# A pooling mixer at the start of a four-layer network: pooled means as products, and its norms by token halves

## The reference, cut to what matters

```
h = rms_norm(x, mix_pre_g[0])
for gi, w in enumerate((2, 4, 8, 16)):              # groups of 256 channels
    mean = trailing sum of h over w tokens / min(t, w)   # t = 1..512
    d[gi] = mean - h
y = einsum('bsgc,gcd->bsgd', d, w_pool) * pool_scale     # a 256x256 product in each group
x = x + rms_norm(y, mix_post_g[0])
f = conv_glu_ffn(rms_norm(x, ffn_pre_g[0]), ...)         # 1024 -> 5632 -> conv -> gated 2816 -> 1024
x = x + rms_norm(f, ffn_post_g[0])
```

## Time and profile before

| | us |
|---|---|
| median of 3 runs | 2565.0 (2564.91 to 2568.99) |
| the profiled execution, whole | 2566.03 |
| its span | 2564.3 |
| busy in the span: PE / PEld / DVE / ACT / POOL | 2349.7 / 1966.1 / 1450.6 / 1061.7 / 491.0 |
| mean granted clock of TensorE | 0.964 |

### The profile page before, as it was taken

One profiled execution on the slowest core, in us unless ns is written; L12 is line 12 of the kernel. 1 busy time (PEld: TensorE's weight loads), 2 busy tenths in 40 slices (PEclk: granted clock), 3 DMA queues, 4 the chain that ended last, 5 costly groups with the idle time before them and its releaser, 6 DMA issues.

```text
span 2564.3 us, 33874 instructions
## 1 busy us (share of the span) xinstructions
PE 2349.7 (92%) x12722; PEld 1966.1 (77%) x12722; DVE 1450.6 (57%) x1972; ACT 1061.7 (41%) x1511; POOL 491.0 (19%) x437
## 2 busy tenths in 40 slices
PE   2699999797889999878798999999999999999998
PEld 2487887675778788767678888888877778988887
DVE  5576578667567857767934533426656652542333
ACT  3454454335555444444234422325446652331331
POOL 3322122232233313224611000011001211000001
PEclk9799999899989999989899999999999999999999
DMA  3154453122225455424311222222211112222221
GB/s 132 47 193 176 175 191 145 66 99 66 83 83 197 166 164 190 154 113 170 128 66 66 103 94 98 99 90 85 101 66 35 52 51 82 99 91 92 96 98 66
DMA packets 55624, 280.06 MB, mean 109 GB/s; under 512 B 7916, under 2 KB 18928, under 8 KB 27616
## 3 DMA queue, kind: packets, MB, share of 16 engines
q1 hardware_dynamic: 33424, 211.45, 22.7%
q0 software_dynamic: 12560, 58.80, 6.6%
q10 hardware_dynamic: 9536, 8.39, 1.0%
HBM read 262.75 MB, written 15.86 MB: 109 GB/s over the span
## 4 chain that ended last, share of the span: by engine, by line
PE 73%; DVE 14%; ACT 5%; issue 4%; POOL 3%; DMA 0%; ACTq 0%; DVEq 0%; POOLq 0%
PE ps L443 21%; PE ps L444 20%; PE ps L445 20%; DVE w_lo L1705 3%; POOL sqsum L2639 2%; ACT w_hi L1034 2%; PE ps L937 1%; PE ps L938 1%; PE ps L939 1%; POOL gl L2720 1%; DVE v L2332 1%; PE ps L971 1%; DVE tg L1770 1%; DVE ada_w L1713 1%; PE ps L710 1%
## 5 line engine op out<-in xcount | busy, mean ns | idle before, releaser
L443 PE MATMUL ps<-h_hi,w_hi 128*128 128x512 f32 (+1 forms) x1984 | 735.5, 371 | 31.7 <-DVE w_lo L1705 17.9
L444 PE MATMUL ps<-h_lo,w_hi 128*128 128x512 f32 (+1 forms) x1984 | 727.3, 367 | 0.0
L445 PE MATMUL ps<-h_hi,w_lo 128*128 128x512 f32 (+1 forms) x1984 | 726.8, 366 | 0.0
L1705 DVE TENSOR_TENSOR w_lo<-raw,w_hi 128x2048 fp32r<-128x2048 f32 x194 | 445.5, 2297 | 465.0 <-ACT w_hi L1034 464.7
L1034 ACT ACTIVATE w_hi<-raw 128x2048 fp32r<-128x2048 f32 x194 | 370.8, 1912 | 387.4 <-PE ps L445 385.1
L443 PEld LDWEIGHTS ps<-h_hi,w_hi 128*128 128x128 f32 x1984 | 381.6, 192 | 102.4 <-issue 17.0
L443 PE MATMUL ps<-a_hi,w_hi 128*128 128x512 f32 (+1 forms) x1164 | 428.7, 368 | 31.3 <-DVE f L2148 14.4
L444 PEld LDWEIGHTS ps<-h_lo,w_hi 128*128 128x128 f32 x1984 | 381.9, 193 | 58.4 <-issue 1.0
L445 PEld LDWEIGHTS ps<-h_hi,w_lo 128*128 128x128 f32 x1984 | 381.8, 192 | 58.4
L444 PE MATMUL ps<-a_lo,w_hi 128*128 128x512 f32 (+1 forms) x1164 | 424.9, 365 | 0.0
L445 PE MATMUL ps<-a_hi,w_lo 128*128 128x512 f32 (+1 forms) x1164 | 424.9, 365 | 0.0
(11 more groups left out here) (382 smaller groups left out, 2671.1 us busy)
## 6 DMA issues: line engine op xcount, KB each, us to landing
raw<-weights_dram SPq DMA_DIRECT2D x161, 1024.0 KB, 4.8
ada_w<-ada_dram POOLq DMA_DIRECT2D x48, 1024.0 KB, 5.1
raw<-weights_dram SPq DMA_DIRECT2D x32, 704.0 KB, 3.9
par<-par_dram SPq DMA_DIRECT2D x8, 1152.0 KB, 7.1
par_dram<-plane POOLq DMA_DIRECT2D x10, 512.0 KB, 3.9
tab<-tab_dram SPq DMA_DIRECT2D x8, 512.0 KB, 5.8
x<-x_in_dram SPq DMA_DIRECT2D x1, 2048.0 KB, 8.9
par_dram<-bt_re ACTq DMA_DIRECT2D x4, 512.0 KB, 3.6
```

The source lines that it names most:

```text
L443: nc.tensor.matmul(dst, w_hi[:, o:o + P], rhs_hi, start=start, stop=False)
L444: nc.tensor.matmul(dst, w_hi[:, o:o + P], rhs_lo, start=False, stop=False)
L445: return nc.tensor.matmul(dst, w_lo[:, o:o + P], rhs_hi, start=False, stop=last)
L1705: nc.vector.tensor_tensor(w_lo[:, o], raw[:, o], w_hi[:, o].bitcast(f32), SUB).then_inc(w_split, 1)
```

## The change

Tokens first: `x_rows`, the input with tokens on the partitions, is loaded in four blocks of 128 tokens ahead of all else; `x` follows behind the first weight tile. ACT squares a block and sums it over its 1024 channels in one operation (`accum_out`), takes the root; VectorE inverts it and scales with it a constant band matrix (128 tokens by 144, for each window: 1/w on the trailing diagonals minus one on the main one; another version for the first 16 tokens). TensorE multiplies each block's 128 channels by that band: f32 products into eight banks, one for each chunk, of which the last 16 columns reach into the next block. The result is d without its channel gain; ACT and VectorE apply the gain as they split it into `dd_hi` and `dd_lo`.

The pooling products run by token halves (256 columns), four groups of half 0, then four of half 1, one bank for each group. The squares of the mix and of `x` are summed on TensorE directly: `start_sum` takes two 128x128 blocks of one squared half chunk by a column of ones, 32 such sums in four norms (m0, x0, m1, x1), in place of POOL's adds. Post norm and the norm of `x` run by halves, and the FFN's first two tiles use `in_pair` with the second half's sums threaded through (`FIRST_HALF`). POOL's two loads wait for the vectors; `cond`'s Silu and the Exp for S5 stand behind the last split of h on ACT. Weights of the pooling tile are split in four parts.

```diff
@@ SP
+        tokens(0)
+        sp.dma_start(band[:, :], consts[:, BAND:BAND + 4 * BW + 64]).then_inc(sem("band_landed"), 16)
+        sp.dma_start(vec[:, 0:gains], vecs[:, 0:gains]).then_inc(sem("band_landed"), 16)
+        for b in range(1, NB):
+            tokens(b)
...
             if name == "pool":
+                sp.dma_start(ident[:, :], consts[:, 0:P]).then_inc(sem("ident_landed"), 16)
+                sp.dma_start(x[:, :], x_in).then_inc(sem("vec_landed"), 16)
+                sp.dma_start(vec[:, gains:], vecs[:, gains:]).then_inc(sem("vec_landed"), 16)
+                sp.dma_start(posi[:, :], pos_in).then_inc(sem("tables_landed"), 16)
...
@@ TensorE
+        def start_sum(name, h, c, b0):
+
+            pe.wait_ge(sem("start_act"), START_STEP[f"{name}_sq{c}"])
+            for b in range(2):
+                o = c % 2 * T + h * TH + b * P
+                last = nc.tensor.matmul(bank(b0 + b, 1), sq[:, o:o + P], ones[:, 0:1], start=(c == 0), stop=(c == DC - 1))
+            last.then_inc(sem("start_pe") if c < DC - 1 else norm_sum_done, 1)
...
+        FIRST_HALF = {**{(0, 0, c + 1): m1_sum(c) for c in range(7)}, (1, 0, 0): m1_sum(7), (1, 0, 2): spread_of[1],
+                      **{(1, 0, c + 3): x1_sum(c) for c in range(5)}, (0, 1, 0): x1_last}
...
+            in_pair((name, name), (2, 2), h_hi, h_lo, hb, LATE_HALF if layer else FIRST_HALF)
...
-        norm_whole()
+        for c in range(DC):
+            nc.tensor.matmul(bank(c), zero_r[:, 0:P], zero_r[:, :], start=True, stop=False)
+        for b in range(NB):
+            pe.wait_ge(sem("start_dve"), START_STEP[f"band{b}"])
+            n = BW if b < NB - 1 else P
+            for c in range(DC):
+                o = c // 2 * BW
+                last = nc.tensor.matmul(bank(c, n, off=b * P), x_tok[:, b * D + c * P:b * D + (c + 1) * P], band_tok[b][:, o:o + n],
+                                        start=False, stop=(b == NB - 1))
...
+        for grp in range(4):
+            mixed(grp, 0)
+            if grp >= 2:
+                for c in (2 * grp - 4, 2 * grp - 3):
+                    start_sum("m0", 0, c, NORM)
+        for c in range(4, DC):
+            start_sum("m0", 0, c, NORM)
+        pe.wait_ge(sem("ident_landed"), 16)
+        for grp in range(4):
+            mixed(grp, 1)
+            if grp == 0:
+                spread_of[0]()
+        for c in range(DC):
+            start_sum("x0", 0, c, SUMS)
+        spread_of[0]()
...
@@ ScalarE
+        for b in range(NB):
+            act.wait_ge(sem(f"tok_landed{b}"), 16)
+            at = start_step(f"sq{b}", nc.scalar.activation(sq[:, :], x_tok[:, b * D:(b + 1) * D], ACT.Square, accum_out=tok_ss[:, b:b + 1]))
+            act.wait_ge(sem("start_act"), at)
+            start_step(f"std{b}", nc.scalar.activation(rcol[:, b:b + 1], tok_ss[:, b:b + 1], ACT.Sqrt, bias=EPS_A, scale=1.0 / D))
...
+        for c in range(DC):
+            act.wait_ge(sem("start_pe"), START_STEP[f"d{c}"])
+            nc.scalar.activation(chunk(dd_hi, c), bank(c), ACT.Identity, scale=v("mix_pre", c)).then_inc(sem("pool_dhi"), 1)
+        split_hi()
+
+        def mixed_square(name, h, c, src, **scaled):
+
+            if c >= 2:
+                act.wait_ge(sem("start_pe"), START_STEP[f"{name}_sum{c - 2}"])
+            start_step(f"{name}_sq{c}", nc.scalar.activation(halved(sq, c % 2, h), src, ACT.Square, **scaled))
...
+        for grp in range(4):
+            act.wait_ge(sem("start_pe"), START_STEP[f"mixed{grp}"])
+            for m in range(2):
+                mixed_square("m0", 0, 2 * grp + m, bank(grp, TH, off=m * TH), scale=v("pool_scale", 2 * grp + m))
+        mixed_copy(0, 0)
+        start_std(0, NORM)
+        for grp in range(1, 4):
+            mixed_copy(grp, 0)
+        for c in range(4):
+            x_square(0, c)
+            mixed_copy(c, 1)
+        x_square(0, 4)
+        g.after()
+        split_hi()
+        for c in range(5, DC):
+            x_square(0, c)
+        start_std(0, SUMS)
+        for c in range(DC):
+            split_halves(0, (c,), h_hi)
+            mixed_square("m1", 1, c, halved(f, c, 1))
+        start_std(1, SUMS)
+        for c in range(DC):
+            x_square(1, c)
+        start_std(1, SUMS)
+        split_halves(1, range(DC), h_hi)
+        act.wait_ge(sem("vec_landed"), 32)
...
@@ VectorE
+        for b in range(NB):
+            dve.wait_ge(sem("start_act"), START_STEP[f"std{b}"])
+            dve.wait_ge(dve_step, mark(nc.vector.reciprocal(rcol[:, b:b + 1], rcol[:, b:b + 1])))
+            ins = nc.vector.tensor_scalar(band_tok[b][:, :], band[:, 0:4 * BW], rcol[:, b:b + 1], None, MUL)
...
+        for c in range(DC):
+            if c % 2 == 0:
+                pool_w_lo(c // 2)
+            dve.wait_ge(sem("pool_dhi"), c + 1)
+            nc.vector.scalar_tensor_tensor(chunk(dd_lo, c), bank(c), v("mix_pre", c), chunk(dd_hi, c).bitcast(f32), MUL, SUB).then_inc(pool_d, 1)
+        split_lo()
+        g.after()
...
+        rstd_of(0)
+        rstd_on_all()
+        post_halves(0, range(DC), mix_gain, 0)
         split_lo()
+        rstd_of(0)
+        rstd_on_all()
...
+        norm_half(0, ffn_gain, h_hi, h_lo)
+        rstd_of(1)
+        rstd_on_all()
+        post_halves(1, range(DC), mix_gain, 4)
+        rstd_of(1)
+        rstd_on_all()
+        norm_half(1, ffn_gain, h_hi, h_lo)
...
@@ GpSimd
+        gp.wait_ge(sem("vec_landed"), 32)
+        gp.dma_start(cond[:, :], c_row).then_inc(sem("c_landed_ada"), 16)
         gp.dma_start(ada_w[:, :], ada[0:P, :]).then_inc(ada_landed, 16)
-        norm_adds()
-        norm_adds()
-        norm_adds()
```

More of the change, by code:

```diff
@@ L88 @@
 ONE_ROWS = HEAD_SEL + 8 * P
+BAND = ONE_ROWS + P
+BW = P + 16
 Q5 = 4
@@ L100, with eight @@
 START = {"mod_kept": 1, "xbc_done": 3}
+def eight(name, n=8):
+    return tuple(f"{name}{c}" for c in range(n))
+START_STEP = {name: k + 1 for names in (
+    ("sq0", "std0", "sq1", "std1", "sq2", "std2", "sq3", "std3", "w_hi0", "w_hi1", "w_hi2")
+    + eight("m0_sq") + eight("x0_sq") + eight("m1_sq") + eight("x1_sq"),
+    eight("d") + eight("mixed", 4) + eight("m0_sum", 7) + eight("x0_sum", 7) + eight("m1_sum", 7) + eight("x1_sum", 7),
+    eight("band", 4) + eight("w_lo", 3)) for k, name in enumerate(names)}
 FULL, FA, FB, XA, XB = "full", "fa", "fb", "xa", "xb"
@@ L144, in rounds, with build @@
         c.r, c.per, c.n = None, 0, c.n0 + n * per
-def build(nc, weights, ada, c_row, vecs, consts, x_in, pos_in, s5_b, s5_c, out):
+def build(nc, weights, ada, c_row, vecs, consts, x_in, x_rows, pos_in, s5_b, s5_c, out):
     f32, f32r, i32 = mybir.dt.float32, mybir.dt.float32r, mybir.dt.int32
@@ L610, in _, with mixed @@
         pe.wait_ge(sem("ones_set"), 1)
-        pe.wait_ge(sem("ident_landed"), 16)
-        norm_whole()
-        pe.wait_ge(w_split, g.after())
-        for grp in range(4):
-            if grp >= 2:
-                pe.wait_ge(pool_out, grp - 1)
+        for c in range(DC):
[7 more added lines that the diff above has]
+                                        start=False, stop=(b == NB - 1))
+                if b == NB - 1:
+                    last.then_inc(sem("start_pe"), 1)
+        def mixed(grp, h):
+            if h:
+                pe.wait_ge(pool_out, grp + 1)
+            elif grp < 3:
+                pe.wait_ge(sem("start_dve"), START_STEP[f"w_lo{grp}"])
+            else:
+                pe.wait_ge(w_split, g.after())
             for m in range(2):
@@ new lines, in start_std, with x_square @@
+        def start_std(h, b0):
+            act.wait_ge(norm_sum_done, C["norm"].after())
+            dst = rcol[:, 2 * h:2 * h + 2].rearrange("p (a o) -> p a o", o=1)
+            nc.scalar.activation(dst, as3(ps[:, b0 * T:(b0 + 2) * T], 2)[:, :, 0:1], ACT.Sqrt, bias=EPS_A).then_inc(std_done, 1)
+        def x_square(h, c):
+            act.wait_ge(x_ready, C["x"].after())
+            mixed_square(f"x{h}", h, c, halved(x, c, h))
+        for grp in range(4):
+            act.wait_ge(sem("start_pe"), START_STEP[f"mixed{grp}"])
+            for m in range(2):
+                mixed_square("m0", 0, 2 * grp + m, bank(grp, TH, off=m * TH), scale=v("pool_scale", 2 * grp + m))
@@ L1782, in norm_half, with post_halves @@
             C["hp"].after(DC)
-        def post_halves(h, chunks, gains):
+        def post_halves(h, chunks, gains, out_at=None):
             steps = []
@@ new lines, in pool_w_lo @@
+        def pool_w_lo(grp):
+            if grp < 3:
+                dve.wait_ge(sem("start_act"), START_STEP[f"w_hi{grp}"])
+            else:
+                dve.wait_ge(w_hi_done, split.after())
+            o = slice(grp * T, (grp + 1) * T)
+            ins = nc.vector.tensor_tensor(w_lo[:, o], raw[:, o], w_hi[:, o].bitcast(f32), SUB)
+            ins.then_inc(sem("start_dve") if grp < 3 else w_split, 1)
+        for c in range(DC):
+            if c % 2 == 0:
+                pool_w_lo(c // 2)
+            dve.wait_ge(sem("pool_dhi"), c + 1)
```

(8 more changed lines are left out.)

159 lines of the change are left out of this document (55 added, 104 removed).

## The result

The changed kernel takes 2539.8 us (median of 4 runs, 2539.4 to 2545.3) against 2566.3 for the kernel before on the same chip: ratio 0.990, interval 0.988 to 0.992, 26.5 us faster. The forecast was 2536 in a range of 2527 to 2553.

A forecast was written before the change was run, and what follows sets the result against it. TensorE's dense stream of products behind a slow start was taken as the bound. The third tile moving from 123.3 to 93.9 saves 29.4 us: 2566.0 to 2536.6, less 1.0 for the median, say 2536; eight in ten 2527 to 2553.

The forecast's parts named there:

- the third tile: Third FFN tile's first product, the yardstick: at 93.9 us instead of 123.3, 29.4 us earlier.
- Input, band products, d: Start: first tokens land at 4.5 us, band 0 ready at 8.4, band products end at 19, d's subtractions at 25.6.
- The wait for the second weight tile: Pooling: tile lands at 25 us, its split takes 1.91, so squares of the pooled output begin at 26.9.
- First norm: Norm of x's first half, ahead of the FFN: reaches VectorE at 50.5 us, against 94.83 before.
- rival (b): TensorE stays at 1.2 GHz through the start: 2562; cold only to x's norm: 2543. Chance 0.15 for 2547 to 2570.
- The mixed stretch: First FFN tile's first half, products with sums between: two chunks at 2.17 us, six at 1.2, ending at 63.7.
- Behind it: Second half's post steps start at 66.2 us, its products at 78.3; third tile 15.57 later; halves cost 43.4 us.
- ACT's late table loads: Exp, Silu and their loads behind h's last split: 3.8 us from 82.0, hidden with 0.5 to spare.
- The rest of the program: From the third tile to the span's end: 2441.0 us as before, within 2 us.
- (c): ACT's squares and TensorE's sums take turns: in addition to a cold start, 19 us more, 2581; chance 0.05.
- (d): The start doesn't set the end because the stream behind hides it: 2565; chance 0.02.
- (a): Clock high and tile early: weights at 23, no cold first sums or FFN chunks: 2529, range 2522 to 2529; chance 0.12.

The follow-up runs named there:

- second profile: Profile from running the changed kernel again, unaltered; it shows an execution of 2539.1 us, where that run's median was 2542.8 us.
- The fifth run: Changed kernel with the second-half mix squares in eight buffers of their own and their sums together behind the first half's FFN products: 2535.1 us, ratio 0.988.
- its repeat: The kernel with the second-half mix sums together behind the first half's FFN products, run again unaltered on the chip of the fillers: 2537.2 us, ratio 0.989.
- the two fillers: Kernel with the second-half mix sums taken out from between FFN products, plus seven idle f32 product pairs there: one column 2549.4 us, 128 columns 2544.0 us.
- front alone: Changed kernel's token blocks and band products, with pooling products, POOL's adds, norms and FFN of the kernel before: 2534.2 us, ratio 0.988.
- halves alone: Front of the kernel before, followed by the change's halves with sums on TensorE and interleaved FFN start: 2575.0 us, ratio 1.0035.
- the wide fillers: Kernel with the second-half mix sums taken out from between FFN products, plus seven idle pairs of 128-column f32 products there: 2544.0 us, ratio 0.991.

## Why the prediction was right, and where it was off

**Sign, size and place held, the size in part by luck.** 26.5 us measured, 29.4 forecast, and the gain lies in the start: 19.0 of the 20.6 us between the two profiled spans stand ahead of the third tile. At that tile, though, the forecast had 29.4, and the two profiles of the change have 19.0 and 23.0. In the second one, whose time of 2539.1 is near the median of 2539.8, 3.8 us more came from behind the tile, where the prediction expected nothing.

**Input, band products, d: right at both ends.** Tokens' first square at 4.75 (forecast 4.5), band 0 ready at 9.1 (8.4), band products through at 19.5 (19), d's first copy at 18.04 (17.2, to 22.3; measured to 22.8), last low half at 25.9 (25.6). In between, the second block of tokens was 2.5 us late, and the low clock lasted to 14 us where the prediction let it end at 12.3. The band's scaling was priced from an operation of another kind, 0.77, and took 0.52.

**The wait for the second weight tile: right.** Landed 24.9 (23.6 in the second profile), forecast 25 between 23 and 27; squares at 26.74, forecast 26.9. The chain of waits names it (DMA of raw from 8.61 for 16.29 us, then the split). That this wait decides was too much said: without it the time changes by 0 to 3 us.

**First norm: right on the mean, open in its cause.** 50.5 forecast, 54.5 and 49.5 measured in two executions of one program, with a granted clock of 0.56 and 0.89 from 26 to 41. I took the low clock for the first sums and a high one from 33.8. The fifth run, its repeat and the two fillers, whose program is the same up to there, have 0.77, 0.54, 0.77 and 0.66. What decides it in one execution isn't settled; the share of rival (b) that says cold up to the norm of x, 7 us late, is what the first profile shows by 4 us.

**The mixed stretch: the term that was mis-sized.** The prediction took two chunks at 2.17 and six at 1.2, 11.5 us, from the second layer, where the clock rises some 4.4 us into the products. Measured: every chunk 2.13, 16.4 us. The price of a cold chunk was right and the clock's rise was not: in the second layer no such sums stand between the products. The fillers show that the one-column sums are the reason. It is rival (b)'s price for this one stretch; (b) as a whole, 1.2 GHz through the start and 2562, did not come: the records run at the high price from 14 to 26 us, and the clock was at 0.97 from 41 to 48 and from 75 to 84.

**Behind it** the intervals held: from VectorE's second post norm to the second half's products 12.7 us (forecast 12.1), from there to the third tile 15.1 (15.6), with the one wait of 1.8 us for w_lo. The halves cost 50 us (49.7 and 50.8 in the two profiles) from VectorE's first product of the norm to the third tile, where 43.4 was charged and the whole form needs 28.4. The prediction had this sum in hand and didn't draw its consequence, that the halves might be worth less than they cost; no rival took the change apart in that way. The runs did: front alone 30.0 us faster, halves alone 10.1 slower, both 21.3 faster.

**ACT's late table loads: right.** Exp and Silu ran from 92.87 to 96.77, the tile's own table load followed at 96.84, and nothing waited. The root started 0.02 us behind the end of its table load (5.91 + 1.28, then 7.21), as in the earlier trace rows. The Trainium skill ("ScalarE: Activation LUTs", "What ACT_TABLE_LOAD costs") would have each switch drain for about 1380 ns more; this trace again doesn't show it.

**The rest of the program** was expected to be equal within 2 us. The first profile keeps to that, the second, by the prediction's own sign, doesn't: from the third tile to the end 2441.0 us before, and 2437.2 to 2440.2 in the twelve profiles after, 2439.5 and 2437.2 in two of the same kernel. This gave back 1.5 to 3.8 us of the miss in front. Only one profile of the kernel before is at hand, so whether the change has a part in it stays open.

**Rivals.** (c), square and sum taking turns, did not come: in the stretch between 56 and 75 TensorE was busy for 18.71 of 19 us. (d) did not either. Of (a) two of three parts came in the second profile, the tile at 23.6 and a clock of 0.89 around the first sums; the third, no cold products in the FFN, did not.

## What to carry to other kernels

A gain that is an engine's idle time filled should be costed at the clock that TensorE has while it does the filling work. In these kernels the one-column sums filled the time and the clock stayed low, so everything between them was paid at nearly twice its price. What helped here was to sum with the ones stationary and the data moving; next best was to keep the one-column sums in one block behind the products, though some 3 us at the low clock followed it. And cost a change of several parts part by part: here one part was worth 30 us and another minus 9 to 10, and the sum hid it.

## What was not expected of the hardware

- The granted clock stayed at 0.50 (1.2 GHz) for 16 us and more although TensorE was shown as busy without a gap, as long as pairs of one-column f32 products stood between every six products of 256 columns; with pairs of 128 columns it rose to 1.00. The Trainium skill ("TensorE: Matmul & The Clock Gate", "Part 1: The HAM clock gate (the "warmup" mystery)") says that the gate follows how busy the engine has been and opens for a busy one. By it the stretch would have taken about the forecast's 11.5 us (an estimate) and not 16.4; the measurement decides.
- A clock that was already high stayed so through the same threading in seven profiles and fell in one: from 75 to 84 us of the first profile, with the second half's sums between products just so, it stayed at 0.97; with the wide fillers, in the same stretch of the program, it fell to 0.50 at 75 us. What decides it isn't shown.
- VectorE's add of 128x512 took 1.10 us while POOL added its squares and 0.68 when it didn't. POOL's own add took 1.63 beside it (13.04 for eight), against 1447 ns on the mean before.
- An inverse of 128x512 on VectorE takes 3.35 us, one of 128x4 0.18, and a product of the same 128x512 with a column and a tensor 0.74.
